# Rows of the moving operands 272 elements apart instead of 256, and the on-chip layout moved to make room

## The chip, the cores and the metric

The kernel runs on one core of one Trainium2 chip. Its time is the device time of one launch in microseconds (us). The kernel before takes 2373.92 us, the median of three runs (2372.8 to 2373.94).

## The reference, cut to what matters

Two transformer-like blocks in float32 on a sequence of 256 tokens with a model width of 2048. What costs time is a row of large products; everything between them is element-wise work on arrays of 256 columns.

```python
# first block, d = 2048, 256 tokens, 256 context tokens
mod = silu(c) @ w_mod                      # 2048 -> 6*2048 (and the same for c_ctx)
hx, hc = modulate(rms_norm(x), ...), modulate(rms_norm(ctx), ...)
q, zf, zb, v = split((hx | hc) @ w_in[:, :4096])      # "rec": both sequences
s_f, s_b = gated scan over the context                # states per head
g, sb, sc, sh, ga, gb = split(hx @ w_in[:, 4096:])    # "mix" and "merge"
y_a, y_b = scan output * silu(g), sb * short_conv(sc * sh)
merged = sigmoid(ga) * (y_a @ w_pa) + sigmoid(gb) * (y_b @ w_pb)   # "merge"
x = x + g1 * (merged @ w_o)                           # "out"
a, b = split(modulate(rms_norm(x)) @ w_up)            # "up", 2048 -> 2*5632
x = x + g2 * ((silu(dwconv3x3(a)) * b) @ w_down)      # "down", 5632 -> 2048
x = rms_norm(x)
# second block: 16 learned tokens put ahead, so 272 tokens
proj = rms_norm(h) @ w_in_2                           # "attn", 2048 -> 8*1024
mixed = [stick_breaking(q, k, v), diff_attention(q, k, v)] * silu(gates)
return h + mixed @ w_out_2                            # "proj"
```

## The kernel before, in words

Activations lie transposed: features on the 128 partitions, tokens along the row. A product of 128 output features is one pass over all blocks k of 128 input features (16 of them; 11 in a product of "down"), and its output is one [128, 256] tile in one of four PSUM banks (ACC).

To reach float32 accuracy, both operands are split into a high part (rounded by the float32r type) and a low part. SyncE loads the weights of a product (1 MB) into RAW, ScalarE copies RAW to HI (L455), VectorE writes LO = RAW - HI (L1135), each in two halves. For every k, `prod` (L744 and following; all its matmuls are recorded at L759) then issues three matmuls into the same bank: HI by the high part of the input, HI by the low part, LO by the high part. Each matmul record has its own weight load of 128 columns (PEld, also L759). The HI and LO tiles hold [2 slots, 16 blocks, 128], so one block of weights is 512 bytes further than the last.

The inputs of products ("moving" operands) are these tiles, with the high and the low part in different slots of the same tile:

- HX [128, 4, 16, 256]: hx and hc, high and low. "rec" reads both sequences at once, as two blocks of 256 columns (512 columns per matmul) for three products per head, and hx alone for the fourth; "mix", "merge" (two of three products) and "up" read hx.
- YAB [128, 4, 8, 256]: y_a and y_b, for the third product of "merge". MRG [128, 2, 16, 256] for "out". SH and SL [128, 44, 256] for "down". MIX [128, 2, 16, 256] for "proj".
- U2 [128, 2, 16, 272]: the input of "attn". Its rows are already 272 elements long. Four of the eight products of a head (p = 0, 3, 6, 7) read columns 16 to 272 of a row, the other four (1, 2, 4, 5) all 272.

The stages follow one another in the order of the list PHASES, as hardware loops: mod1 (vector by matrix, weights streamed), rec (8 heads of 4 products), mix (8 heads of 4), merge (16 columns of 3), out (16 products), up (88), down (64 products of 11 blocks), attn (8 heads of 8), proj (16). In rec, merge and out VectorE also does one unit each of `mod_unit` (L1145): a [128, 2048] multiply and sum straight from RAW.

A product waits for a free bank, for its LO halves and in some stages for its inputs. SyncE loads a weight unit as soon as the LO two units ahead of it has read the buffer. Every on-chip tile has a fixed address: `at(name, kb, shape)` gives it the offset base + kb * 1024 bytes, with base = 16512; so tiles of different stages lie over each other, and the order of the stages and semaphores keep them apart. The first 16 KB below are the scratch in which descriptors of DMAs that GpSimd issues are built. GpSimd issues six DMAs in all: 1 MB to the tensor park in HBM early on and back into CROWB ahead of merge, 2 MB of X1 to park after out, 2 MB back into XF and the 16 learned tokens when up has ended, and constants ahead of attn.

Of the kernel before, what the change touches and what calls it, by code (L numbers as in the profile page):

```python
# [8 lines left out]
F32R = mybir.dt.float32r  # L9
# [5 lines left out]
P = 128  # L15
# [107 lines left out]
def build(nc, xct, metat, crow, vec, con1, con2, wts, wdown, park, outt):  # L123
    ctx = ExitStack()
    with ctx:
        base = 16512

# [10 lines left out]

        HX = at("hx", 64, [P, 4, KD, T], F32R)
        YAB = at("yab", 96, [P, 4, HEADS, T], F32R)  # L140
        XC = at("xc", 128, [P, 2, KD, T])
        SQ1 = at("sq1", 160, [P, 2, 4, 2, T])
        SS1 = at("ss1", 194, [P, 2, T])
        RAWX = at("rawx", 48, [P, 2, 16, P])
        CS32 = at("cs32", 182, [P, KD, 32])
        ROW = at("row", 168, [P, 2, 4 * P])
        RS1 = at("rs1", 176, [P, 2, T])
        N1 = at("n1", 178, [P, 2, 2, T])
        FG = at("fg", 144, [P, 2, HEADS, T])
        VT = at("vt", 160, [P, 2, HEADS * P])  # L150
        ST = at("st", 168, [P, 2, HEADS, P])
        QF = at("qf", 176, [P, HEADS, T])
        MRG = at("mrg", 144, [P, 2, KD, T], F32R)
        X1 = at("x1", 128, [P, KD, T])
        SH = at("sh", 96, [P, FF, T], F32R)
        SL = at("sl", 140, [P, FF, T], F32R)
        XF = at("xf", 64, [P, KD, T])
        U2 = at("u2", 96, [P, 2, KD, TA], F32R)
        MIX = at("mix", 130, [P, 2, 2 * HEADS, T], F32R)
        CON2 = at("con2", 162, [P, NC2])  # L160

        CON1 = at("con1", 184 + 13.5, [P, NC1])
        cbase = 184 + 13.5 + NC1 / 256
        VEC = at("vec", cbase, [P, NVEC])
# [7 lines left out]

        SG = at("sg", 128, [P, 2, 2, T])
        FC = at("fc", 132, [P, 2, T])
        EXC = at("exc", 136, [P, 2, T])
        KDT = at("kdt", 138, [P, 4, P])
        VS = at("vs", 140, [P, 2, T])
        VCT = at("vct", 142, [P, 2, P])
        SGQ = at("sgq", 143, [P, T])
        ONE = at("one", 184, [P, T])  # L180

        CROW = at("crow_all", 185, [P, D])
        CROWB = at("crow_b", 176, [P, D])
        CGATE = at("cgate", 160, [P, D])

        AR = at("ar", 128, [P, 4, T])
        TT0 = at("tt0", 132, [P, 3, T])
        QK = at("qk", 135, [P, 4, T])
        QLA = at("qla", 139, [P, 2, 2, T])
        KS = at("ks", 143, [P, T])  # L190
        TT1 = at("tt1", 184, [P, 3, P])
        QLB = at("qlb", 185.5, [P, 1, 2, T])
        ON = at("on", 187.5, [P, 2, P])
        YT = at("yt", 188.5, [P, T])
        SC = at("sc", 189.5, [P, 2, T])
        QS = at("qs", 191.5, [P, 2, T])

        GS = at("gs", 193.5, [P, T])
        SGG = at("sgg", 194.5, [P, T])
        UP = at("up", 195.5, [P, T + 8])  # L200
        SCB = at("scb", cbase + 4.625, [P, T])

        GA = at("ga", 184, [P, T])
        GB = at("gb", 185, [P, T])
        M1 = at("m1", 186, [P, T])
        M2 = at("m2", 187, [P, T])

        SQ2 = at("sq2", 190, [P, 2, T])
        ZERO = at("zero", 196.25, [P, T])
        RS2 = at("rs2", 187, [P, T])  # L210
        N2 = at("n2", 188, [P, 8, T])

        AT = at("at", 184, [P, 6, GRID + 2])
        CV = at("cv", 185.75, [P, T])
        CV2 = at("cv2", 186.75, [P, T])
        S1 = at("s1", 187.75, [P, T])

        SQ3 = at("sq3", 192, [P, 2, 2, T])
        RSF = at("rsf", 190, [P, T])

# [3 lines left out]
        SQMS = at("sqms", 83, [P, NMETA])  # L224
        RTOK = at("rtok", 184, [P, TA])
        SGB = at("sgb", 185.25, [P, T])
        SGD = at("sgd", 186.25, [P, T])
        a0 = 80
# [10 lines left out]
        GDF = at("gdf", a0 + 14.5625, [P, T])  # L239
        b0 = 162 + NC2 / 256  # L240
        SS = at("ss", b0, [P, 2, P + NMETA + TA])
# [513 lines left out]
        def _(pe):  # L755
# [50 lines left out]
            pe.wait_ge(c_silu, 1)  # L806
            xch, xcl = (lambda k: HX[:, 0:3:2, k, :]), (lambda k: HX[:, 1:4:2, k, :])

# [30 lines left out]
            def rec_head(i, peeled):  # L839
# [5 lines left out]
                def turns():  # L845
# [9 lines left out]
                    for s in range(2):  # L855
# [3 lines left out]

                prod("rec", i, 6, lambda k: HX[:, 0, k, :], lambda k: HX[:, 1, k, :], lambda k: ACC[:, 3, 0:T],  # L860
                     between=turns)
# [60 lines left out]
            def mix_head(i, peeled):  # L922

                xh, xl = (lambda k: HX[:, 0, k, :]), (lambda k: HX[:, 1, k, :])

                prod("mix", i, 0, xh, xl, lambda k: ACC[:, 0, 0:T], between=None if peeled else lambda: mix_level(i - 1, 7))
                if not peeled:
                    mix_outputs(i - 1)
                mix_same(i)
                mix_level(i, 0)  # L930
                prod("mix", i, 1, xh, xl, lambda k: ACC[:, 1, 0:T], between=lambda: mix_level(i, 1))
                if not peeled:
                    mix_turn(i - 1)
# [9 lines left out]
            def merge_columns(i, peeled=False):  # L943

                xh, xl = (lambda k: HX[:, 0, k, :]), (lambda k: HX[:, 1, k, :])
                for jj in range(4):
# [7 lines left out]
                    if first:  # L954
                        mix_turn(HEADS - 1, True)
                        pe.wait_ge(yb_ready, 1 + HEADS)

                    prod("merge", i, p + 2, lambda k: YAB[:, 2 - 2 * (k // 8), k % 8, :], lambda k: YAB[:, 3 - 2 * (k // 8), k % 8, :],
                         lambda k: ACC[:, (b + 2) % 4, (1 - k // 8) * T:(2 - k // 8) * T], lambda k: (k % 8 == 0, k % 8 == 7),
# [8 lines left out]
            with pe.Fori(0, ITERS["out"]) as i:  # L968
# [5 lines left out]
                for jj in range(4):  # L974
                    prod("out", i, 2 * jj, lambda k: MRG[:, 0, k, :], lambda k: MRG[:, 1, k, :], lambda k: ACC[:, jj, 0:T],
                         between=lambda: squares(jj - 1), inputs=mrg_ready if jj == 0 else None, each=4)
# [3 lines left out]
            with pe.Fori(0, ITERS["up"]) as i:  # L980
                for p in range(4):
                    prod("up", i, p, lambda k: HX[:, 0, k, :], lambda k: HX[:, 1, k, :], lambda k: ACC[:, p, 0:T],
                         inputs=hx2_ready if p == 0 else None)
# [4 lines left out]
            with pe.Fori(0, ITERS["down"]) as i:  # L988
# [9 lines left out]
                for jj in range(2):  # L998
                    for q in range(4):
                        p = 4 * jj + q  # L1000
                        u = prod_index("down", i, p)
                        if jj == 0:
                            pe.wait_ge(s_hidden, 1 + DT * (q + 1))
                        prod("down", i, p, lambda k: SH[:, DT * q + k, :], lambda k: SL[:, DT * q + k, :],
                             lambda k: ACC[:, jj, 0:T], lambda k: (q == 0 and k == 0, q == 3 and k == DT - 1),
# [106 lines left out]
            with pe.Fori(0, ITERS["proj"]) as i:  # L1112
                for p in range(4):
                    prod("proj", i, p, lambda k: MIX[:, 0, k, :], lambda k: MIX[:, 1, k, :], lambda k: ACC[:, p, 0:T],
                         inputs=mix_ready, needs=head_order if p == 0 else {KD: 0})
# [3 lines left out]
        def _(dve):  # L1119
# [73 lines left out]
            def inputs(j):  # L1193

                dve.wait_ge(h1_aff, j + 1)
                hh, hl = HX[:, 0:3:2, j, :], HX[:, 1:4:2, j, :]
                link(V.tensor_copy(hh, N1[:, j % 2]))
# [102 lines left out]
            def mix_ya(i):  # L1300

                x = lambda d: YAB[:, d, bass.ds(i, 1), :].rearrange("p a t -> p (a t)")
                dve.wait_ge(on_tr, i + 1)
# [22 lines left out]
            def mix_head(i, peeled):  # L1326
# [26 lines left out]

                x = lambda d: YAB[:, d, bass.ds(i, 1), :].rearrange("p a t -> p (a t)")
                qf = QF[:, bass.ds(i, 1), :].rearrange("p a t -> p (a t)")
# [56 lines left out]
            def merge_columns(i, peeled=False):  # L1412

                for jj in range(4):
# [21 lines left out]
                    dve.wait_ge(bank_free, prod_index("merge", i, p + 2) + 1)  # L1436
                    o = lambda s: MRG[:, s, bass.ds(j, 1), :].rearrange("p a t -> p (a t)")
                    link(V.tensor_copy(o(0), M1[:]))
# [25 lines left out]
            for g in range(5):  # L1464
# [3 lines left out]
                if g > 0:  # L1468
                    n = N2[:, 4 * ((g - 1) % 2):4 * ((g - 1) % 2) + 4, :]
                    dve.wait_ge(h2_aff, g)  # L1470
                    split_small(HX[:, 0, 4 * g - 4:4 * g, :], HX[:, 1, 4 * g - 4:4 * g, :], n).then_inc(hx2_ready, 1)
                    dve.wait_ge(hx2_ready, g)
# [4 lines left out]
            with dve.Fori(0, ITERS["up"]) as i:  # L1477
                ch.enter(i, CHAIN["v_up"])
                for jj in range(2):
# [28 lines left out]
                    dve.wait_ge(bank_free, prod_index("up", i, 2 * jj + 1) + 1)  # L1508
                    o = lambda t: t[:, bass.ds(j, 1), :].rearrange("p a t -> p (a t)")
                    split_small(o(SH), o(SL), CV2[:]).then_inc(s_hidden, 1)  # L1510
# [82 lines left out]
            def attn_head(i, peeled):  # L1593
# [6 lines left out]
                def mixed(g):  # L1600
                    o = lambda s: MIX[:, s, bass.ds(2 * i + 1 - g, 1), :].rearrange("p a t -> p (a t)")
                    split_small(o(0), o(1), MT[:]).then_inc(mix_ready, 1)
# [222 lines left out]
```

## Time and profile before

| what | value |
|---|---|
| median of 3 runs | 2373.92 us |
| the profiled execution's own time | 2372.26 us |
| its span, first to last instruction | 2370.5 us |
| TensorE matmul busy | 2303.0 us, 97% of the span |
| VectorE, ScalarE busy | 1632.6 us (69%), 983.3 us (41%) |
| mean granted TensorE clock | 0.992 |
| DMA queues | 201 GB/s over the span |

A busy share is the share of the span in which at least one instruction of that engine was in work. Matmuls are pipelined: the duration of one (some 280 ns at 256 columns) is its time from start to modelled end, while the next one starts long before that. What a matmul costs in a stream is therefore the distance between two starts: divide a stretch by the number of matmuls in it.

Inside the span, rec runs in the window 137 to 421 us, mix in 455 to 655, merge in 672 to 945, out in 945 to 1044, up in 1062 to 1560, down in 1572 to 1834, attn in 1834 to 2275 and proj in 2275 to 2370; a window leaves the seams between stages out.

### The profile page before, as it was taken

How to read it: one execution, taken by the hardware profiler on the slowest of the kernel's cores; microseconds unless marked ns; L12 is line 12 of the kernel's file. 1: busy time of each engine (PE TensorE's matmuls, PEld its weight loads, DVE VectorE, ACT ScalarE, POOL GpSimd, SP SyncE). 2: the span in 40 equal slices, each digit the busy share in tenths (PEclk: the TensorE clock that was granted, in tenths of full speed). 3: DMA queues.
4: the chain of work that ended last, by engine and by line, in shares of the span. 5: the costliest groups of instructions: out<-in, count | busy, mean ns of one | idle time of the engine just before them, and what ended most of it. 6: DMA issues, size and time to landing. Idle time of an engine off the chain costs nothing.

```text
span 2370.5 us, 48809 instructions
## 1 busy us (share of the span) xinstructions
PE 2303.0 (97%) x18474; PEld 2221.4 (94%) x18474; DVE 1632.6 (69%) x2522; ACT 983.3 (41%) x1370; POOL 8.4 (0%) x18
## 2 busy tenths in 40 slices
PE   3899999999999999989999999999999999999999
PEld 2688888999999999989999999999999999999999
DVE  3465556999976666888888778864455766666764
ACT  4223222545533334344444444444344544444442
POOL 0000000000000000000000000000000000000000
PEclk8999999999999999999999999999999999999999
DMA  9965555433356667875444454455555444344443
GB/s 398 399 231 212 204 220 191 182 128 138 134 217 240 243 239 289 330 281 189 177 177 185 187 182 189 178 184 182 171 170 191 164 157 162 144 157 155 146 175 127
DMA packets 69511, 475.62 MB, mean 201 GB/s; under 512 B 7728, under 2 KB 9776, under 8 KB 18384
## 3 DMA queue, kind: packets, MB, share of 16 engines
q1 hardware_dynamic: 68688, 467.59, 52.6%
q0 software_dynamic: 768, 7.26, 0.8%
q8 instruction: 39, 0.64, 0.1%
q14 instruction: 16, 0.13, 0.0%
HBM read 469.58 MB, written 5.24 MB: 200 GB/s over the span
## 4 chain that ended last, share of the span: by engine, by line
PE 84%; DVE 8%; DMA 4%; issue 2%; ACT 1%; DVEq 1%; SPq 0%; ACTq 0%
PE acc L759 80%; PE aux L759 4%; DMA raw<-wts 4%; DVE lo L1135 3%; DVE ar L1352 2%; DVE qla L1345 1%; DVE sc L1324 1%; DVE tt L1350 1%; DVE qlb L1345 0%; PE aux L1030 0%; DVE yab L1151 0%; ACT hi L455 0%; DVE yab L1152 0%; DVE hx L1152 0%; ACT n L630 0%
## 5 line engine op out<-in xcount | busy, mean ns | idle before, releaser
L759 PE MATMUL acc<-hx,hi 128*128 128x256 f32 (+1 forms) x5888 | 1174.2, 299 | 11.5 <-DVE hx L1152 8.5
L759 PEld LDWEIGHTS acc<-hx,hi 128*128 128x128 f32 x5888 | 942.8, 192 | 45.8 <-issue 13.9
L1135 DVE TENSOR_TENSOR lo<-raw,hi 128x1024 fp32r<-128x1024 f32 (+1 forms) x716 | 811.1, 1167 | 218.7 <-ACT hi L455 214.4
L759 PE MATMUL acc<-hx,lo 128*128 128x256 f32 (+1 forms) x2944 | 875.1, 297 | 0.0
L455 ACT ACTIVATE hi<-raw 128x1024 fp32r<-128x1024 f32 (+1 forms) x716 | 694.6, 1010 | 330.0 <-PE acc L759 272.5
L759 PEld LDWEIGHTS acc<-hx,lo 128*128 128x128 f32 x2944 | 564.1, 192 | 15.6
L759 PE MATMUL acc<-u,hi 128*128 128x272 f32 (+1 forms) x2048 | 384.0, 288 | 0.0
L759 PEld LDWEIGHTS acc<-u,hi 128*128 128x128 f32 x2048 | 318.6, 188 | 4.5 <-issue 2.5
L759 PE MATMUL acc<-u,lo 128*128 128x256 f32 (+1 forms) x1024 | 291.6, 285 | 0.0
L759 PE MATMUL acc<-sh,hi 128*128 128x256 f32 x704 | 202.4, 288 | 0.4 <-DVE lo L1135 0.4
L759 PE MATMUL acc<-sh,lo 128*128 128x256 f32 x704 | 199.3, 283 | 0.0
L759 PE MATMUL acc<-sl,hi 128*128 128x256 f32 x704 | 199.2, 283 | 0.0
L759 PEld LDWEIGHTS acc<-u,lo 128*128 128x128 f32 x1024 | 193.0, 188 | 0.0
L759 PEld LDWEIGHTS acc<-sh,hi 128*128 128x128 f32 x704 | 135.1, 192 | 1.1 <-DVE lo L1135 0.6
L759 PEld LDWEIGHTS acc<-sl,hi 128*128 128x128 f32 x704 | 135.1, 192 | 0.4
L759 PEld LDWEIGHTS acc<-sh,lo 128*128 128x128 f32 x704 | 135.0, 192 | 0.0
L1501 DVE SCALAR_TENSOR_TENSOR cv<-at,vec,cv 128x256 f32<-128x256 f32 x308 | 129.1, 477 | 0.0
L759 PE MATMUL acc<-mrg,hi 128*128 128x256 f32 x512 | 95.7, 288 | 0.0
L759 PE MATMUL acc<-yab,hi 128*128 128x256 f32 x512 | 92.9, 283 | 0.0
L759 PE MATMUL acc<-mix,hi 128*128 128x256 f32 x512 | 92.3, 283 | 0.0
L759 PEld LDWEIGHTS acc<-mrg,hi 128*128 128x128 f32 x512 | 80.7, 191 | 0.9
L759 PEld LDWEIGHTS acc<-yab,hi 128*128 128x128 f32 x512 | 79.9, 192 | 0.2 <-issue 0.2
(286 smaller groups left out, 1979.1 us busy)
## 6 DMA issues: line engine op xcount, KB each, us to landing
raw<-wts SPq DMA_DIRECT2D x390, 1024.0 KB, 4.8
raw<-wdown SPq DMA_DIRECT2D x64, 704.0 KB, 4.1
xc<-xct SPq DMA_DIRECT2D x1, 4096.0 KB, 12.6
rawx<-wts SPq DMA_DIRECT2D x2, 1024.0 KB, 27.7
x<-xct SPq DMA_DIRECT2D x1, 2048.0 KB, 10.6
park<-x POOLq DMA_DIRECT2D x1, 2048.0 KB, 8.7
xf<-park POOLq DMA_DIRECT2D x1, 2048.0 KB, 10.6
outt<-outs SPq DMA_DIRECT2D x16, 128.0 KB, 3.9
```

The source lines that it names most:

```text
L455: A.activation(HI[:, slot, a:b, :], RAW[:, p % 4, a:b, :], ACT.Copy).then_inc(hi_half, 1)
L759: return pe.matmul(*a, **k)
L1135: V.tensor_tensor(LO[:, slot, a:b, :], RAW[:, p % 4, a:b, :], HI[:, slot, a:b, :].bitcast(F32), ALU.subtract).then_inc(lo_half, 1)
L1324: V.copy_predicated(SC4[:, 0:4:3, :], m, AUX[:, bank, 0:T].rearrange("p (t n) -> p t n", t=2)).then_inc(tile_read, 1)
L1345: V.tensor_tensor(q, ar, qk, ALU.mult).then_inc(ql_ready, 1)
L1350: mark(V.tensor_tensor(bass.AP(after[:].tensor, 0, [[3 * (P, T)[l % 2], P], [1, 3 * blocks // 2]]), even, odd, ALU.mult))
L1352: mark(V.tensor_tensor(ar, ar, tt, ALU.mult))
L1501: mark(V.scalar_tensor_tensor(acc4[n % 2], a, w, acc4[n % 2], ALU.mult, ALU.add))
```

## The change

All moving operands get rows of TW = 272 elements, of which only the first 256 are written and read. HX and YAB, MRG, MIX, SH and SL grow by a sixteenth each. "up" reads its input through a new name, HXU, of two slots over the same place as HX. To make the room, the scratch for DMAs of GpSimd is set to 8192 bytes (by default the base of 16512 left 16384), the base of all tiles goes 8192 bytes down, and most tiles after YAB get kb values 8 higher, so that their absolute addresses stay; X1, MRG, SL, AT, CV, CV2, S1 and ZERO go elsewhere. The loops, the order of instructions, the semaphores and the number and shape of all operations are the same.

```diff
+TW = T + NMETA
-        base = 16512
+        base = 8320
-        HX = at("hx", 64, [P, 4, KD, T], F32R)
-        YAB = at("yab", 96, [P, 4, HEADS, T], F32R)
-        XC = at("xc", 128, [P, 2, KD, T])
+        HX = at("hx", 64, [P, 4, KD, TW], F32R)
+        YAB = at("yab", 98, [P, 4, HEADS, TW], F32R)
+        XC = at("xc", 136, [P, 2, KD, T])
...
-        MRG = at("mrg", 144, [P, 2, KD, T], F32R)
-        X1 = at("x1", 128, [P, KD, T])
-        SH = at("sh", 96, [P, FF, T], F32R)
-        SL = at("sl", 140, [P, FF, T], F32R)
+        MRG = at("mrg", 150, [P, 2, KD, TW], F32R)
+        X1 = at("x1", 134, [P, KD, T])
+        HXU = at("hxu", 64, [P, 2, KD, TW], F32R)
+        SH = at("sh", 98, [P, FF, TW], F32R)
+        SL = at("sl", 144.75, [P, FF, TW], F32R)
         XF = at("xf", 64, [P, KD, T])
         U2 = at("u2", 96, [P, 2, KD, TA], F32R)
-        MIX = at("mix", 130, [P, 2, 2 * HEADS, T], F32R)
+        MIX = at("mix", 130, [P, 2, 2 * HEADS, TW], F32R)
...
-        ZERO = at("zero", 196.25, [P, T])
+        ZERO = at("zero", cbase + 4.625, [P, T])
-        AT = at("at", 184, [P, 6, GRID + 2])
+        AT = at("at", 200, [P, 6, GRID + 2])
...
-            xch, xcl = (lambda k: HX[:, 0:3:2, k, :]), (lambda k: HX[:, 1:4:2, k, :])
+            xch, xcl = (lambda k: HX[:, 0:3:2, k, 0:T]), (lambda k: HX[:, 1:4:2, k, 0:T])
...
-                    prod("up", i, p, lambda k: HX[:, 0, k, :], lambda k: HX[:, 1, k, :], lambda k: ACC[:, p, 0:T],
+                    prod("up", i, p, lambda k: HXU[:, 0, k, 0:T], lambda k: HXU[:, 1, k, 0:T], lambda k: ACC[:, p, 0:T],
...
-                    split_small(HX[:, 0, 4 * g - 4:4 * g, :], HX[:, 1, 4 * g - 4:4 * g, :], n).then_inc(hx2_ready, 1)
+                    split_small(HXU[:, 0, 4 * g - 4:4 * g, 0:T], HXU[:, 1, 4 * g - 4:4 * g, 0:T], n).then_inc(hx2_ready, 1)
...
-    nc = bacc.Bacc("TRN2", target_bir_lowering=False, num_devices=1)
+    nc = bacc.Bacc("TRN2", target_bir_lowering=False, num_devices=1, dynamic_dma_scratch_size=8192)
```

All other reads and writes of these tiles change in the same way, from `:` to `0:T`.

## Rows read from the trace of the kernel before

**Rows 1.** The page: busy time by engine; the chain that ended last, by engine.

```profile
PE 2303.0 (97%) x18474; PEld 2221.4 (94%) x18474; DVE 1632.6 (69%) x2522; ACT 983.3 (41%) x1370; POOL 8.4 (0%) x18
...
PE 84%; DVE 8%; DMA 4%; issue 2%; ACT 1%; DVEq 1%; SPq 0%; ACTq 0%
```

**Rows 2.** Windows: us, busy of PE, PEld, DVE, ACT, POOL, PEclk, DMA share, GB/s.

```profile
137.00:421.00 284.00, 284.00 (x1481) 244.40 (x1480) 168.33 (x215) 73.80 (x94) 0.00 (x0) 1.00 0.56 212
...
455.00:655.00 200.00, 193.82 (x1607) 190.38 (x1606) 189.91 (x340) 102.87 (x170) 3.16 (x6) 1.00 0.37 137
...
672.00:945.00 273.00, 272.71 (x2271) 272.32 (x2271) 176.33 (x208) 109.01 (x136) 0.00 (x0) 1.00 0.66 250
945.00:1044.00 99.00, 99.00 (x803) 98.11 (x802) 81.19 (x84) 37.17 (x47) 0.00 (x0) 1.00 0.89 334
...
1062.00:1560.00 498.00, 498.00 (x4151) 497.87 (x4150) 397.37 (x692) 221.43 (x305) 0.00 (x0) 1.00 0.48 180
...
1572.00:1834.00 262.00, 262.00 (x2135) 260.27 (x2134) 130.69 (x166) 109.62 (x155) 0.33 (x1) 1.00 0.53 182
1834.00:2275.00 441.00, 439.67 (x3465) 426.42 (x3463) 306.10 (x516) 207.06 (x302) 0.21 (x1) 1.00 0.41 155
```

**Rows 3.** The chain in order of time: start us, us, what (rec, merge, up, down, proj).

```profile
141.75 35.56 PE acc L759 x168
...
738.28 210.22 PE acc L759 x1752
...
1061.66 497.25 PE acc L759 x4140
...
1573.16 15.83 PE acc L759 x132
...
2275.54 92.36 PE acc L759 x768
```

**Rows 4.** Timeline of PE in "up": start us, us, instruction; twelve blocks k lie between.

```profile
1099.74 0.40 PE L759 MATMUL acc<-hx,hi 128*128 128x256 f32 x2
...
1104.06 0.40 PE L759 MATMUL acc<-hx,hi 128*128 128x256 f32 x2
```

**Rows 5.** Timeline of PE in "attn", seventh product (p = 6), blocks k = 9 to 15.

```profile
1933.70 0.40 PE L759 MATMUL acc<-u,hi 128*128 128x256 f32 x2
...
1934.06 0.40 PE L759 MATMUL acc<-u,hi 128*128 128x256 f32 x2
...
1934.41 0.40 PE L759 MATMUL acc<-u,hi 128*128 128x256 f32 x2
...
1934.77 0.40 PE L759 MATMUL acc<-u,hi 128*128 128x256 f32 x2
...
1935.83 0.40 PE L759 MATMUL acc<-u,hi 128*128 128x256 f32 x2
```

**Rows 6.** The same, first blocks of the product after a stop (p = 7).

```profile
1939.49 0.28 PE L759 MATMUL acc<-u,lo 128*128 128x256 f32 x1
...
1940.88 0.28 PE L759 MATMUL acc<-u,lo 128*128 128x256 f32 x1
```

**Rows 7.** The same, a product of 272 columns from column 0 (p = 2).

```profile
1957.79 0.41 PE L759 MATMUL acc<-u,hi 128*128 128x272 f32 x2
...
1958.92 0.42 PE L759 MATMUL acc<-u,hi 128*128 128x272 f32 x2
...
1959.31 0.41 PE L759 MATMUL acc<-u,hi 128*128 128x272 f32 x2
...
1963.46 0.42 PE L759 MATMUL acc<-u,hi 128*128 128x272 f32 x2
```

**Rows 8.** DVE between out and up, by shape: busy us, mean ns.

```profile
L1151 DVE CAST hx<-n 128x1024 fp32r<-128x1024 f32 x4 | 2.8, 690 | 1.4 <-ACT n L630 1.4
```

**Rows 9.** DMA issues of GpSimd: KB, us to landing; who DVE's L1557 waited for.

```profile
xf<-park POOLq DMA_DIRECT2D x1, 2048.0 KB, 10.6
...
DVE xf L1557 <- PE acc L759: 25.8, 15, 2.6
```

More of the change, by code:

```diff
@@ L137, in build @@
         LO = at("lo", 48, [P, 2, 16, P], F32R)
-        HX = at("hx", 64, [P, 4, KD, T], F32R)
-        YAB = at("yab", 96, [P, 4, HEADS, T], F32R)
-        XC = at("xc", 128, [P, 2, KD, T])
-        SQ1 = at("sq1", 160, [P, 2, 4, 2, T])
-        SS1 = at("ss1", 194, [P, 2, T])
-        RAWX = at("rawx", 48, [P, 2, 16, P])
[L145 to L152, printed above, removed]
-        MRG = at("mrg", 144, [P, 2, KD, T], F32R)
-        X1 = at("x1", 128, [P, KD, T])
-        SH = at("sh", 96, [P, FF, T], F32R)
-        SL = at("sl", 140, [P, FF, T], F32R)
+        HX = at("hx", 64, [P, 4, KD, TW], F32R)
+        YAB = at("yab", 98, [P, 4, HEADS, TW], F32R)
+        XC = at("xc", 136, [P, 2, KD, T])
+        SQ1 = at("sq1", 168, [P, 2, 4, 2, T])
+        SS1 = at("ss1", 202, [P, 2, T])
+        RAWX = at("rawx", 48, [P, 2, 16, P])
+        CS32 = at("cs32", 190, [P, KD, 32])
+        ROW = at("row", 176, [P, 2, 4 * P])
+        RS1 = at("rs1", 184, [P, 2, T])
+        N1 = at("n1", 186, [P, 2, 2, T])
+        FG = at("fg", 152, [P, 2, HEADS, T])
+        VT = at("vt", 168, [P, 2, HEADS * P])
+        ST = at("st", 176, [P, 2, HEADS, P])
+        QF = at("qf", 184, [P, HEADS, T])
+        MRG = at("mrg", 150, [P, 2, KD, TW], F32R)
[3 more added lines that the diff above has]
+        SL = at("sl", 144.75, [P, FF, TW], F32R)
         XF = at("xf", 64, [P, KD, T])
         U2 = at("u2", 96, [P, 2, KD, TA], F32R)
-        MIX = at("mix", 130, [P, 2, 2 * HEADS, T], F32R)
-        CON2 = at("con2", 162, [P, NC2])
-        CON1 = at("con1", 184 + 13.5, [P, NC1])
-        cbase = 184 + 13.5 + NC1 / 256
+        MIX = at("mix", 130, [P, 2, 2 * HEADS, TW], F32R)
+        CON2 = at("con2", 170, [P, NC2])
+        CON1 = at("con1", 192 + 13.5, [P, NC1])
+        cbase = 192 + 13.5 + NC1 / 256
         VEC = at("vec", cbase, [P, NVEC])
@@ L171, in build @@
         SMALL = at("small", cbase + 4.5, [P, 32])
[L173 to L200, printed above, removed]
@@ L201, in build @@
-        SCB = at("scb", cbase + 4.625, [P, T])
[L203 to L208, printed above, removed]
-        ZERO = at("zero", 196.25, [P, T])
-        RS2 = at("rs2", 187, [P, T])
-        N2 = at("n2", 188, [P, 8, T])
-        AT = at("at", 184, [P, 6, GRID + 2])
-        CV = at("cv", 185.75, [P, T])
-        CV2 = at("cv2", 186.75, [P, T])
-        S1 = at("s1", 187.75, [P, T])
@@ L218, in build @@
-        SQ3 = at("sq3", 192, [P, 2, 2, T])
-        RSF = at("rsf", 190, [P, T])
+        SG = at("sg", 136, [P, 2, 2, T])
+        FC = at("fc", 140, [P, 2, T])
+        EXC = at("exc", 144, [P, 2, T])
+        KDT = at("kdt", 146, [P, 4, P])
+        VS = at("vs", 148, [P, 2, T])
+        VCT = at("vct", 150, [P, 2, P])
+        SGQ = at("sgq", 151, [P, T])
+        ONE = at("one", 192, [P, T])
+        CROW = at("crow_all", 193, [P, D])
+        CROWB = at("crow_b", 184, [P, D])
+        CGATE = at("cgate", 168, [P, D])
@@ new lines, in build @@
+        AR = at("ar", 136, [P, 4, T])
+        TT0 = at("tt0", 140, [P, 3, T])
+        QK = at("qk", 143, [P, 4, T])
+        QLA = at("qla", 147, [P, 2, 2, T])
+        KS = at("ks", 151, [P, T])
+        TT1 = at("tt1", 192, [P, 3, P])
+        QLB = at("qlb", 193.5, [P, 1, 2, T])
+        ON = at("on", 195.5, [P, 2, P])
+        YT = at("yt", 196.5, [P, T])
+        SC = at("sc", 197.5, [P, 2, T])
+        QS = at("qs", 199.5, [P, 2, T])
+        GS = at("gs", 201.5, [P, T])
+        SGG = at("sgg", 202.5, [P, T])
@@ new lines, in build @@
+        UP = at("up", 203.5, [P, T + 8])
+        SCB = at("scb", cbase + 4.625, [P, T])
+        GA = at("ga", 192, [P, T])
+        GB = at("gb", 193, [P, T])
+        M1 = at("m1", 194, [P, T])
+        M2 = at("m2", 195, [P, T])
+        SQ2 = at("sq2", 198, [P, 2, T])
+        ZERO = at("zero", cbase + 4.625, [P, T])
+        RS2 = at("rs2", 195, [P, T])
+        N2 = at("n2", 196, [P, 8, T])
+        AT = at("at", 200, [P, 6, GRID + 2])
+        CV = at("cv", 201.75, [P, T])
+        CV2 = at("cv2", 202.75, [P, T])
@@ L221, in build @@
+        S1 = at("s1", 203.75, [P, T])
+        SQ3 = at("sq3", 200, [P, 2, 2, T])
+        RSF = at("rsf", 198, [P, T])
         METT = at("mett", 80, [P, KD, NMETA])
@@ L224, in build @@
         SQMS = at("sqms", 83, [P, NMETA])
-        RTOK = at("rtok", 184, [P, TA])
-        SGB = at("sgb", 185.25, [P, T])
-        SGD = at("sgd", 186.25, [P, T])
+        RTOK = at("rtok", 192, [P, TA])
+        SGB = at("sgb", 193.25, [P, T])
+        SGD = at("sgd", 194.25, [P, T])
         a0 = 80
@@ L239, in build @@
         GDF = at("gdf", a0 + 14.5625, [P, T])
-        b0 = 162 + NC2 / 256
+        b0 = 170 + NC2 / 256
         SS = at("ss", b0, [P, 2, P + NMETA + TA])
@@ L858, in turns @@
                     ins.then_inc(v_tr, 1)
-                prod("rec", i, 6, lambda k: HX[:, 0, k, :], lambda k: HX[:, 1, k, :], lambda k: ACC[:, 3, 0:T],
+                prod("rec", i, 6, lambda k: HX[:, 0, k, 0:T], lambda k: HX[:, 1, k, 0:T], lambda k: ACC[:, 3, 0:T],
                      between=turns)
@@ L922, in mix_head @@
             def mix_head(i, peeled):
-                xh, xl = (lambda k: HX[:, 0, k, :]), (lambda k: HX[:, 1, k, :])
+                xh, xl = (lambda k: HX[:, 0, k, 0:T]), (lambda k: HX[:, 1, k, 0:T])
                 prod("mix", i, 0, xh, xl, lambda k: ACC[:, 0, 0:T], between=None if peeled else lambda: mix_level(i - 1, 7))
@@ L943, in merge_columns @@
             def merge_columns(i, peeled=False):
-                xh, xl = (lambda k: HX[:, 0, k, :]), (lambda k: HX[:, 1, k, :])
+                xh, xl = (lambda k: HX[:, 0, k, 0:T]), (lambda k: HX[:, 1, k, 0:T])
                 for jj in range(4):
@@ L956, in merge_columns @@
                         pe.wait_ge(yb_ready, 1 + HEADS)
-                    prod("merge", i, p + 2, lambda k: YAB[:, 2 - 2 * (k // 8), k % 8, :], lambda k: YAB[:, 3 - 2 * (k // 8), k % 8, :],
+                    prod("merge", i, p + 2, lambda k: YAB[:, 2 - 2 * (k // 8), k % 8, 0:T], lambda k: YAB[:, 3 - 2 * (k // 8), k % 8, 0:T],
                          lambda k: ACC[:, (b + 2) % 4, (1 - k // 8) * T:(2 - k // 8) * T], lambda k: (k % 8 == 0, k % 8 == 7),
@@ L974, in _ @@
                 for jj in range(4):
-                    prod("out", i, 2 * jj, lambda k: MRG[:, 0, k, :], lambda k: MRG[:, 1, k, :], lambda k: ACC[:, jj, 0:T],
+                    prod("out", i, 2 * jj, lambda k: MRG[:, 0, k, 0:T], lambda k: MRG[:, 1, k, 0:T], lambda k: ACC[:, jj, 0:T],
                          between=lambda: squares(jj - 1), inputs=mrg_ready if jj == 0 else None, each=4)
@@ L1003, in _ @@
                             pe.wait_ge(s_hidden, 1 + DT * (q + 1))
-                        prod("down", i, p, lambda k: SH[:, DT * q + k, :], lambda k: SL[:, DT * q + k, :],
+                        prod("down", i, p, lambda k: SH[:, DT * q + k, 0:T], lambda k: SL[:, DT * q + k, 0:T],
                              lambda k: ACC[:, jj, 0:T], lambda k: (q == 0 and k == 0, q == 3 and k == DT - 1),
@@ L1113, in _ @@
                 for p in range(4):
-                    prod("proj", i, p, lambda k: MIX[:, 0, k, :], lambda k: MIX[:, 1, k, :], lambda k: ACC[:, p, 0:T],
+                    prod("proj", i, p, lambda k: MIX[:, 0, k, 0:T], lambda k: MIX[:, 1, k, 0:T], lambda k: ACC[:, p, 0:T],
                          inputs=mix_ready, needs=head_order if p == 0 else {KD: 0})
@@ L1195, in inputs @@
                 dve.wait_ge(h1_aff, j + 1)
-                hh, hl = HX[:, 0:3:2, j, :], HX[:, 1:4:2, j, :]
+                hh, hl = HX[:, 0:3:2, j, 0:T], HX[:, 1:4:2, j, 0:T]
                 link(V.tensor_copy(hh, N1[:, j % 2]))
@@ L1300, in mix_ya @@
             def mix_ya(i):
-                x = lambda d: YAB[:, d, bass.ds(i, 1), :].rearrange("p a t -> p (a t)")
+                x = lambda d: YAB[:, d, bass.ds(i, 1), 0:T].rearrange("p a t -> p (a t)")
                 dve.wait_ge(on_tr, i + 1)
@@ L1352, in level @@
                     mark(V.tensor_tensor(ar, ar, tt, ALU.mult))
-                x = lambda d: YAB[:, d, bass.ds(i, 1), :].rearrange("p a t -> p (a t)")
+                x = lambda d: YAB[:, d, bass.ds(i, 1), 0:T].rearrange("p a t -> p (a t)")
                 qf = QF[:, bass.ds(i, 1), :].rearrange("p a t -> p (a t)")
@@ L1436, in merge_columns @@
                     dve.wait_ge(bank_free, prod_index("merge", i, p + 2) + 1)
-                    o = lambda s: MRG[:, s, bass.ds(j, 1), :].rearrange("p a t -> p (a t)")
+                    o = lambda s: MRG[:, s, bass.ds(j, 1), 0:T].rearrange("p a t -> p (a t)")
                     link(V.tensor_copy(o(0), M1[:]))
@@ L1508, in _ @@
                     dve.wait_ge(bank_free, prod_index("up", i, 2 * jj + 1) + 1)
-                    o = lambda t: t[:, bass.ds(j, 1), :].rearrange("p a t -> p (a t)")
+                    o = lambda t: t[:, bass.ds(j, 1), 0:T].rearrange("p a t -> p (a t)")
                     split_small(o(SH), o(SL), CV2[:]).then_inc(s_hidden, 1)
@@ L1600, in mixed @@
                 def mixed(g):
-                    o = lambda s: MIX[:, s, bass.ds(2 * i + 1 - g, 1), :].rearrange("p a t -> p (a t)")
+                    o = lambda s: MIX[:, s, bass.ds(2 * i + 1 - g, 1), 0:T].rearrange("p a t -> p (a t)")
                     split_small(o(0), o(1), MT[:]).then_inc(mix_ready, 1)
```

## The prediction

> **What bounds the kernel now.** I read the page first: TensorE is busy in 97% of the span, and 84% of the chain that ended last is its work [rows 1]. The windows by stage then say where that is a limit and where it is only company [rows 2]. In rec, merge, out, up, down and attn TensorE is busy in nearly all of the stretch while VectorE is busy in half to just over four fifths of it (in up 397 of 498 us, in out 81 of 99). In mix TensorE is busy 193.8 of 200 us, but VectorE is busy 189.9 of the same 200, in 340 short instructions that depend on one another: I read it as VectorE setting the pace there. DMA is far from full but for out, with 334 GB/s in a share of 0.89.
>
> So the figure that matters is the distance between the starts of two matmuls in a stream. The chain gives it: 210.22 us for 1752 matmuls in merge, 120.0 ns; 497.25 for 4140 in up, 120.1; 15.83 for 132 in down, 119.9; 92.36 for 768 in proj, 120.3 with its last drain [rows 3]. In "up" twelve blocks of three take 4.32 us, 120.0 ns each [rows 4]. Four stages with quite different work on the other engines and different DMA traffic have one and the same figure, so neither those engines nor the DMAs set it. What a column costs comes from rec: 168 matmuls in 35.56 us, of which 144 have 512 columns and 24 have 256; 35.56 less 24 x 0.120 is 32.68, over 144 is 226.9 ns [rows 3]. So 256 columns more cost 106.9 ns, 0.418 ns each, one column per cycle of the 2.4 GHz level (granted clock 1.00 in these windows [rows 2]). A matmul of 256 columns at 120.0 ns thus carries 13.0 ns that are not columns. The change can only touch these.
>
> **The change, part by part.**
>
> *The pitch.* The kernel before has the case already: U2 has rows of 272 elements, everything else rows of 256. In attn, matmuls of 256 columns from U2, well inside a product, take 2.13 us for 18, 118.3 ns [rows 5]. They are the same instructions as in up: three per block, same weights tiles, same banks, same clock. The steps between blocks show more: 0.36, 0.35, 0.36 us, where up has 0.36 on the mean of twelve [rows 4, 5]. At 256 elements (1024 bytes) each row starts at the same place modulo any smaller power of two, as the weights do, which lie 512 bytes apart; at 272 (1088 bytes) each row starts 64 bytes further against the weights. I take the 13.0 ns to be in part a clash between the stream of the input and the load of the next weights that depends on their relative place, and the 1.7 ns to be what walking through four places (64 bytes x 4 = 256) gains on standing at the worst or near it.
>
> The new reads start at column 0, those of U2 at column 16, that is 64 bytes on: one step of the walk. Over four blocks they visit the same places. The distance from high to low slot, 16 x 1088 bytes in HX, is a multiple of 256 as in U2; for SH to SL it is 46.75 KB, also one; 8192 bytes off all bases changes nothing in this count. So I put the rate of rows 5 on all changed tiles.
>
> Other rows bound it. After a stop, the first blocks from U2 run at 1.39 us for 12, 115.8 ns [rows 6]: gain 4.2. Products of 272 columns from column 0 take 5.67 us for 45, 126.0 ns [rows 7]; less 16 columns at 0.418 that is 119.3: gain 0.7. The latter starts at column 0 as the new reads do but is longer, the former reading is of the right length; I take 1.7 because length decides when the next load falls into the stream, and the start is only a shift of the walk. The inner ends are 0.7 and 4.2.
>
> *How many matmuls.* From the loops: rec 8 x 48 = 384 of 256 columns and 8 x 144 = 1152 of 512; merge 16 x 3 x 48 = 2304; out 768; up 88 x 48 = 4224; down 64 x 33 = 2112; proj 768. That is 10,560 of 256 columns. Mix has 1536 more, which I count at nothing: VectorE's chain covers them, and a quicker product there only makes TensorE wait longer [rows 2]. For the 512-column ones no row has the new pitch; the load is hidden behind the same one matmul, so I give them the same 1.7 (ends: 0 and 4.2, since twice the columns may halve or double what clashes). Attn keeps its tile, its reads and, modulo 256, its address: nothing.
>
> Sum: 10,560 x 1.7 = 18.0 us, by stage: up 7.2, merge 3.9, down 3.6, out 1.3, proj 1.3, rec 0.7. And 1152 x 1.7 = 2.0. Together 20.0 us.
>
> A sentence of the Trainium skill speaks against this. Its page "SBUF — State Buffer", section "Who interferes with whom", gives TensorE two independent read ports, one for the moving operand and one for weight loads, and says that TensorE never waits on anyone. By it the pitch could not matter, and the time would stay. The trace doesn't sit well with that: 120.0 against 118.3 ns for the same instruction with only the tile's pitch and start different [rows 4, 5].
>
> *What is late next.* At 118.3 ns a pair of products of up takes 11.36 us instead of 11.52. VectorE is busy 397 of 498 us there, 9.2 us per pair; it keeps 2 us of slack. Out loads 2 MB per column: 334 GB/s become 339. Nothing else comes near.
>
> *VectorE and ScalarE.* Writes to the tiles by single rows keep their shape. Between out and up four copies of 1024 elements go into HX as four rows now with holes; they take 690 ns each [rows 8]. If holes cost them a faster mode they would take up to twice that, 4 x 0.7 = 2.8 us on the path, since TensorE waits there; copies into two separate blocks exist elsewhere, so I take 0, ends 0 and 2.8.
>
> *The halved scratch.* Only six DMAs of GpSimd use it. The one with least room is xf from park: 10.6 us to landing [rows 9], issued at the end of up, needed after the first four products of down, about 4 x 4 = 16 us later; in the trace VectorE waits there for TensorE and not for the DMA [rows 9]. Should the smaller ring force the DMA into two turns, 21 us instead of 10.6 would make it late by 5 us, once. I take 0, ends 0 and 5.
>
> Total: 2372.26 - 20.0 = 2352.3 for an execution like the profiled one (span 2370.5 and 1.8 around it). The median lies 1.66 higher, so 2354.0.
>
> **The rivals.**
>
> (a) *The weaker reading of the pitch*: 0.7 ns a matmul, as rows 7 give it. 11,712 x 0.7 = 8.2 us: 2365.7. For it: these rows start at column 0. Against: rows 5 are the same shape as the new ones.
>
> (b) *No change*: the 1.7 ns belong to something else in attn, say stops of the queue that let weight loads run ahead. For it: after a stop the rate is better [rows 6], and attn has many stops. Against: rows 5 lie nine blocks and more after the last stop, and down, where each column of products has a stop in it, is back at 119.9 within a product [rows 3]. Time 2373.9.
>
> (c) *Slower*: the walk through the places isn't an average that wins but has a bad step, and the new tiles sit in it more than U2 does. In rows 7 the step from 1958.92 to 1959.31 is 130 ns a matmul, 123.3 after taking off 16 columns: 3.3 ns over the standing 120. If the changed tiles had that step throughout, 11,712 x 3.3 = 39 us: 2413; it decides from a mean above 120.0 on. For it: one step in four is that long. Against: four steps together are still under 120 in both shapes of attn, and the new tiles walk the same four.
>
> (d) *More*: streams from column 0 keep the rate of rows 6 all the way: 11,712 x 4.2 = 49 us, 2325. Nothing but the first blocks after a stop shows it.
>
> **How the numbers follow.** Forecast (gain 1.2 to 2.6 ns, 2343 to 2360) 0.60; (a) 0.14; (d) or a part of it 0.09; (b) 0.10; (c) or a ring or copy that costs more than the pitch gives 0.07. A measurement of this kernel tells a change from none at about 0.2%, 4.7 us; so faster has 0.60 + 0.14 + 0.09 = 0.83, same 0.10, slower 0.07. The range leaves out (b) and (c) at 0.17 and the far part of (d): 2335 to 2369.
>
> **What would show it.** Right: the chain's stretches in up, merge, down and proj come to 118 to 118.5 ns a matmul, with steps between blocks that alternate; attn's stretches stay as they are; mix keeps its length, with a little more waiting of TensorE; copies at L1151 stay at 690 ns; L1557 still waits for TensorE. Wrong: up at 120.0 (then pitch isn't the cause), or up quicker and attn slower (then it is the base), or mix shorter too (then VectorE wasn't its limit).

## The result, and the profile after

The changed kernel takes 2360.11 us (median of 5, 2359.81 to 2360.93) against 2373.47 for the kernel before (2372.59 to 2373.94): a ratio of 0.9946 with a 95% interval of 0.9932 to 0.9959, 13.4 us less. The forecast was 2354.0, 20 us less, with 2335 to 2369 as its range. The direction was right and the gain is two thirds of what was forecast. The time alone lies between the forecast and rival (a), 2365.7; the rates per matmul below tell the two apart.

The chain of waits of the changed kernel, in order of time (start us, us, what), answers to [rows 3]. A line of it is called a piece below: a stretch of TensorE's work with no wait in it that the profile shows.

```profile
142.01 36.18 PE acc L761 x168
...
742.02 207.32 PE acc L761 x1752
...
1061.57 490.37 PE acc L761 x4140
...
1566.07 15.62 PE acc L761 x132
...
2265.20 91.09 PE acc L761 x768
```

Divide again: merge 118.3 ns a matmul (120.0 before), up 118.4 (120.1), down 118.3 (119.9), proj 118.6 (120.3). But rec, whose pieces of 168 hold 144 matmuls of 512 columns, went the other way: 36.18 us instead of 35.56. Less 24 of 118.3 ns, the 512-column ones take 231.5 ns; before it was 226.9.

The start times of the same pieces tell how the difference to before builds up: +0.3 us at the first of rec, +3.7 at the long one of merge, -0.1 at that of up, -7.1 at the first of down, -10.3 at proj, and -11.6 at the end of the span (2358.9 against 2370.5). The medians lie 13.4 apart; these two traces hold 11.6 of it. The seven pieces of 168 in rec lose 7 x 0.62 = 4.3 us, mix is as long as it was, and the start of merge gives 0.9 back by the second of these marks; the rest of merge and out give 3.8, up 7.0, down and attn 3.3, proj 1.3. Attn itself stays as it was: 436.8 us from its first piece to the start of proj's in both kernels.

The timeline of TensorE in up, blocks twelve apart and two between (start us, us, instruction), answers to [rows 4]. Three matmuls make a block; the steps now alternate as those of U2 did in [rows 5], and twelve of them take 4.26 us, 118.3 ns each:

```profile
1099.85 0.40 PE L761 MATMUL acc<-hxu,hi 128*128 128x256 f32 x2
...
1100.20 0.40 PE L761 MATMUL acc<-hxu,hi 128*128 128x256 f32 x2
...
1100.56 0.40 PE L761 MATMUL acc<-hxu,hi 128*128 128x256 f32 x2
...
1104.11 0.40 PE L761 MATMUL acc<-hxu,hi 128*128 128x256 f32 x2
```

The groups by shape between out and up, then VectorE's waits and GpSimd's DMAs, answer to [rows 8, 9]. The copies keep their 690 ns, the waits at the place where xf is needed still name TensorE, and the DMA takes 10.9 us:

```profile
L1153 DVE CAST hxu<-n 128x1024 fp32r<-128x1024 f32 x4 | 2.8, 690 | 1.4 <-ACT n L632 1.4
```

```profile
DVE xf L1559 <- PE acc L761: 24.7, 15, 2.5
```

```profile
xf<-park POOLq DMA_DIRECT2D x1, 2048.0 KB, 10.9
```

### The profile page after: what moved, and what is told of

Its sections match the earlier page's. It is cut to its first block, busy times and chain, and to the rows that moved or that the text cites. A ratio compares the mean times of both kernels' runs of the same rounds, so it can differ in the third digit from the quotient of the medians.

```text
span 2358.9 us, 48809 instructions
## 1 busy us (share of the span) xinstructions
PE 2291.3 (97%) x18474; PEld 2203.9 (93%) x18474; DVE 1633.4 (69%) x2522; ACT 984.5 (42%) x1370; POOL 8.4 (0%) x18
## 4 chain that ended last, share of the span: by engine, by line
PE 84%; DVE 9%; DMA 4%; issue 2%; ACT 1%; DVEq 1%; SPq 0%; ACTq 0%
PE acc L761 79%; PE aux L761 4%; DMA raw<-wts 4%; DVE lo L1137 3%; DVE ar L1354 2%; DVE qla L1347 1%; DVE sc L1326 1%; DVE tt L1352 1%; DVE qlb L1347 0%; PE aux L1032 0%; ACT hi L457 0%; DVE yab L1153 0%; DVE yab L1154 0%; DVE hxu L1154 0%; ACT n L632 0%
## 5 line engine op out<-in xcount | busy, mean ns | idle before, releaser
L761 PE MATMUL acc<-hx,hi 128*128 128x256 f32 (+1 forms) x3072 | 663.4, 312 | 2.8 <-DVE lo L1137 2.3
L761 PEld LDWEIGHTS acc<-hx,hi 128*128 128x128 f32 x3072 | 497.7, 189 | 39.7 <-issue 5.3
L761 PE MATMUL acc<-hxu,hi 128*128 128x256 f32 x2816 | 502.0, 281 | 8.4 <-DVE hxu L1154 8.2
L761 PE MATMUL acc<-hx,lo 128*128 128x256 f32 (+1 forms) x1536 | 476.2, 310 | 0.0
L761 PEld LDWEIGHTS acc<-hxu,hi 128*128 128x128 f32 x2816 | 433.5, 189 | 9.5 <-issue 8.2
L761 PE MATMUL acc<-hxu,lo 128*128 128x256 f32 x1408 | 396.8, 282 | 0.0
L761 PEld LDWEIGHTS acc<-hx,lo 128*128 128x128 f32 x1536 | 291.0, 189 | 16.6
L761 PEld LDWEIGHTS acc<-hxu,lo 128*128 128x128 f32 x1408 | 267.4, 190 | 0.0
## 6 DMA issues: line engine op xcount, KB each, us to landing
x<-xct SPq DMA_DIRECT2D x1, 2048.0 KB, 10.3
xf<-park POOLq DMA_DIRECT2D x1, 2048.0 KB, 10.9
```

The lines of the kernel that those rows point to most:

```text
L761: return pe.matmul(*a, **k)
```

## The experiments

The question was what of the pitch matters: that rows walk, or where they stand against the weights. Below, the "place" of a tile is the distance in bytes of its row starts from the row starts of HI and LO, modulo 256. Rows 256 elements apart all have one place; rows of 272 walk over 0, 64, 128 and 192. Experiments 1 to 6, 8 to 10 and 12 were run once each, so what they say is read from the lengths of their pieces, and not from a few us of the total.

**1. Base alone.** `base = 8320` and the halved scratch, all rows still 256 elements.

> The kernel before with the halved scratch and all tiles 8192 bytes lower, rows still 256 elements. Theory A (the pitch alone moved the time): 256-column matmuls stand at 120.0 ns in up, 512-column ones at 226.9 in rec, time within 0.1% of before, 2373 us. Theory B (the base or the smaller scratch does part of it): rec gets longer by up to 5 us or up gets quicker already here.

Measured 2373.7 us, with 2373.28 for the kernel before beside it; up 497.25 us for 4140 matmuls as before. Theory B falls: base and scratch change nothing that can be seen.

**2 and 3. A constant shift.** As 1, with rows of 256 elements, and every tile but the four of the weights 64 or 128 bytes on. (The edit for 64 bytes; base and scratch as in 1 are left out.)

```diff
-            return nc.alloc_sbuf_tensor_at(name, shape, dt, offset=base + int(kb * 1024))
+            return nc.alloc_sbuf_tensor_at(name, shape, dt, offset=base + int(kb * 1024) + (0 if name in ("raw", "hi", "lo", "rawx") else 64))
```

> As e1, and every tile but RAW, HI, LO and RAWX lies 64 bytes further, so that every moving row of 256 elements starts 64 bytes (modulo 256) from where the weights' rows start. Theory A1 (the relative place of stream and weight load sets the cost): all 256-column matmuls of hx, sh, sl, mrg, yab and mix leave 120.0 ns together and stand at one new figure between 113 and 122; at 118.3 the time is about 2354, and the 512-column ones move as well. Theory C (walking from row to row matters, a constant shift doesn't): 120.0 and 226.9 as before, 2373 us.

> As e2 with 128 bytes. Theory A1: another constant figure than at 0 and at 64 bytes; the mean over the four places 0, 64, 128 and 192 should lie near the 118.3 of the walk, so with 120.0 at 0 at least one of 64 and 128 is under 118.3. Theory C: 120.0 and 2373 us.

Measured 2351.31 and 2368.01 us against 2373.28. Without any change of pitch, 64 bytes give 22 us, more than the change itself. Theory C (only walking matters) falls. The first piece of rec and the long one of up, at 64 bytes:

```profile
141.62 35.69 PE acc L759 x168
...
181.91 35.80 PE acc L759 x168
...
1056.24 488.08 PE acc L759 x4140
```

and at 128 bytes:

```profile
144.85 36.30 PE acc L759 x168
...
1066.41 491.75 PE acc L759 x4140
```

Up stands at 117.9 and 118.8 ns. Rec is longer at both.

**4. The weights moved along.** As 2, with RAW, HI, LO and RAWX 64 bytes on too.

> As e2, but RAW, HI, LO and RAWX are moved by the same 64 bytes, so that nothing changes in relation. Theory A1 (relative place): 120.0 and 226.9 again, 2373 us. Theory D (the absolute place of the stream matters, not that of the weights): the same figures as in e2.

Measured 2372.57 us; all is as before:

```profile
142.02 35.56 PE acc L759 x168
...
1061.94 497.25 PE acc L759 x4140
```

So it is not the address of the moving rows but their distance from the weight tiles. Theory D falls. With experiment 2 this is the central pair of this case. It doesn't tell yet which of the shifted tiles counts, since those of the other engines moved too; experiments 7 and 10 do, below.

**5, 6, 8 and 9. More places.** The same edit with 192, 32, 224 and 160 bytes.

> The kernel before (rows of 256 elements) with the halved scratch, all tiles but RAW, HI, LO and RAWX 192 bytes further. Constant places 0, 64 and 128 gave 120.0, 117.7 and about 118.7 ns for a matmul of 256 columns. Theory A1 (a walk costs the mean of its four places, 118.3): 192 bytes must give 4 x 118.3 - 120.0 - 117.7 - 118.7 = 116.8 ns, time 2373 - 10560 x 3.2 = about 2340, unless the 512-column ones get worse. Rival A2 (the order of the places in a walk has a cost of its own, so that no mean holds): another figure, 118 to 120.

> As e5 with 32 bytes. Theory A3 (only the place in units of 64 bytes counts): 120.0 as at 0, or 117.7 as at 64. Theory A4 (a finer pattern): a figure of its own between or beside them. No forecast of the sign beyond that; 2351 to 2374.

> As the 192-byte run, with 224 bytes. Constant places gave in up 120.0 (0), 116.7 (32), 117.8 (64), 118.7 (128) and 113.3 ns (192), in rec 226.9, 233.3, 229.2, 232.4 and 233.3. If the cost follows the place smoothly, 224 lies between 113.3 and 120.0 in up and the time between 2327 and 2374; if it is a pattern with jumps, anything, 113.3 or 120.0 among it.

> As above with 160 bytes, between 128 (118.7) and 192 (113.3). Smooth: about 116 ns in up, 2345 us. In jumps: 113.3 or over 118.

Measured 2326.71, 2345.98, 2362.76 and 2368.73 us (2373.24 and 2372.24 for before beside them). The chain at 192 bytes (rec, merge, up, two products' stretches of down, proj):

```profile
182.63 36.34 PE acc L759 x168
...
740.51 206.35 PE acc L759 x1752
...
1057.31 469.76 PE acc L759 x4140
...
1540.90 15.55 PE acc L759 x132
...
1557.32 14.98 PE acc L759 x132
...
2235.09 87.27 PE acc L759 x768
```

and the piece of up at 32, 224 and 160 bytes:

```profile
1058.00 483.50 PE acc L759 x4140
```

```profile
1064.02 490.37 PE acc L759 x4140
```

```profile
1068.34 491.75 PE acc L759 x4140
```

| place, bytes | 0 | 32 | 64 | 128 | 160 | 192 | 224 | walk (the change) |
|---|---|---|---|---|---|---|---|---|
| up, ns a matmul (piece / 4140) | 120.1 | 116.8 | 117.9 | 118.8 | 118.8 | 113.5 | 118.4 | 118.4 |
| rec, us per 168 | 35.56 | 36.40 | 35.69 to 35.80 | 36.30 | 36.58 | 36.34 to 36.44 | 36.44 | 36.18 |
| total, us | 2373.7 | 2346.0 | 2351.3 | 2368.0 | 2368.7 | 2326.7 | 2362.8 | 2360.1 |

Place 0, where the kernel before stood, is the worst in up for 256 columns and the best of all for 512. Places 32 bytes apart differ, so theory A3 falls. The relation is not smooth: 160 costs what 128 does, and nothing between 128 and 192. The expectation that a walk costs the mean of its four places failed as well (117.6 from 120.1, 117.9, 118.8 and 113.5; it costs 118.4).

The table's row for up is one stage in one execution per place, and a place does not fix the rate by itself. At 160 bytes other stages of the same execution ran at other rates: merge at 120.0 ns, as at place 0, proj at 117.6, and the pieces of down in turn at 117.3, 120.0 and twice 118.6:

```profile
746.63 210.24 PE acc L759 x1752
...
1574.26 15.49 PE acc L759 x132
...
1590.61 15.84 PE acc L759 x132
...
2274.02 90.32 PE acc L759 x768
```

It is not the clock: rec, merge, up, down and proj have a granted clock of 1.00 in every trace. The other places but 0 and 224 show it too. At 64 bytes the 24 matmuls of 256 columns that end a piece of rec come at 113.3 ns in one head and at 117.9 in the next, which is the difference between its 35.69 and 35.80 us (below: the first of them and the instruction behind the last, in the two heads). At 128 the first piece of down took 15.84 us and the others 15.66; at 32 proj took 118.0 ns where up took 116.8.

```profile
174.43 0.39 PE L759 MATMUL acc<-hx,hi 128*128 128x256 f32 x2
...
177.15 0.60 PE L851 MATMUL aux<-con,exc 128*128 128x128 f32 x4
...
214.72 0.40 PE L759 MATMUL acc<-hx,hi 128*128 128x256 f32 x2
...
217.55 0.60 PE L851 MATMUL aux<-con,exc 128*128 128x128 f32 x4
```

At 192 bytes the modelled duration of a matmul is shorter as well. The groups by shape in up (1100 to 1500 us: busy us, mean ns), 192 bytes first, then the kernel before:

```profile
L759 PE MATMUL acc<-hx,hi 128*128 128x256 f32 x2354 | 400.2, 276 | 0.0
...
L759 PEld LDWEIGHTS acc<-hx,hi 128*128 128x128 f32 x2354 | 354.6, 188 | 0.0
```

```profile
L759 PE MATMUL acc<-hx,hi 128*128 128x256 f32 x2224 | 400.4, 283 | 0.0
...
L759 PEld LDWEIGHTS acc<-hx,hi 128*128 128x128 f32 x2223 | 346.8, 192 | 0.0
```

A matmul lasts 276 ns instead of 283, a weight load 188 instead of 192: about as much as the 6.7 ns between the two rates lies within the matmul's own duration, and at place 0 the load is longer too. A clash of the two would look like this, but the ends of matmuls are modelled, so these rows don't show it.

**7. HX alone back to 256 in the changed kernel.** Up reads through HXU, whose rows stay at 272.

```diff
-        HX = at("hx", 64, [P, 4, KD, TW], F32R)
+        HX = at("hx", 64, [P, 4, KD, T], F32R)
```

> The changed kernel with HX alone back at rows of 256 elements (place 0); all other tiles keep 272. If the 512-column matmuls of rec are what the change loses (231.7 against 226.9 ns by its trace), rec shortens by 4.9 us against the change, merge, whose products of hx stand at 120.0 again, gets longer by 1536 x 1.7 = 2.6, mix stays: 2357.8 against 2360.1 of the change. Rival (the loss in rec comes from the base or from the tiles moved with it): rec stays as long as in the change and the time is 2362 to 2363.

Measured 2358.84 us (2358.81 to 2359.43), ratio to before 0.9941 (0.9924 to 0.9958). Expected were 2357.8. Rec is back, and merge is 1.9 us longer, as its products of hx at the old rate should make it:

```profile
141.83 35.56 PE acc L761 x168
...
738.29 209.24 PE acc L761 x1752
...
1059.78 490.38 PE acc L761 x4140
```

From piece to piece of the two kernels, the long one of merge starts 3.7 us earlier than in the change and that of up 1.8 us earlier. The loss in rec comes from the reads of HX at the new pitch, nothing else that moved.

**10 and 11. Each tile at its better place.** Rows of 256 elements; HX at place 0 for rec, mix and merge, a name HXU of its own, 192 bytes further on, for up, and all other tiles but those of the weights at 192. (Base and scratch as in 1, and the reads and writes of up, which go to HXU, are left out.)

```diff
+            return nc.alloc_sbuf_tensor_at(name, shape, dt, offset=base + int(kb * 1024) + (0 if name in ("raw", "hi", "lo", "rawx", "hx") else 192))
...
+        HXU = at("hxu", 64, [P, 2, KD, T], F32R)
```

> HX at place 0 (rec, mix, and the products of hx in merge), its use in up and all other moving tiles at place 192, rows of 256 elements. If places act tile by tile: rec as before (512 columns at 226.9, 358 us in all against 363 at 192), merge's 1536 matmuls of hx at 120.0 again where 192 bytes had 116 on the mean (6 us more), up at 113.3, total within 2 us of the 2326.7 of the 192-byte run. Rival: the 113.3 ns of up hang on all tiles standing alike, then up falls back to 117 or more and the time is over 2340.

> The kernel of the tenth run again (HX at place 0, all other moving tiles at place 192, rows of 256), timed against the kernel before in five rounds. From its one time, 2322.93 against 2372.24: ratio 0.979, 2323 us. Its gain over the change (2360.1) should come from up (483 against 504 us), down, rec, merge, out and proj.

The tenth run gave 2322.93 us, 3.8 under the fifth, where at most 2 were expected: merge did not get longer (206.25 us for the piece, against 206.35), because its products of YAB ran at 113.6 ns here and nearly all at 117.8 in the fifth. Every tile but HX stands here as in the fifth run, and rec is back at 35.53 us; so the place of the tile that TensorE reads counts, not that of the other engines' tiles.

Timed in the eleventh: 2324.26 us (median of 6) against 2372.45, ratio 0.9811 with a 95% interval of 0.9788 to 0.9835. This version beats the kernel before by 48 us and, by the medians, the change by 36. But one of its six executions took 2342.73 us, where the others took 2322.7 to 2326.5. Up alone at 117.8 instead of 113.3 ns would give 4224 x 4.5 = 19 us more, an estimate that fits the 18; no trace of that execution was kept, so its cause is not shown. The gain of place 192 is thus not certain in every execution.

The chain in rec, merge, up and proj of an execution of 2323.2 us:

```profile
141.58 35.53 PE acc L760 x168
...
737.00 206.25 PE acc L760 x1752
...
1053.79 469.76 PE acc L760 x4140
...
2231.57 87.27 PE acc L760 x768
```

**12. Two rates at one place.** In down of the eleventh kernel the stretches between two sums of squares alternate, 15.55 and 14.98 us for the same 132 matmuls:

```profile
1569.63 15.55 PE acc L760 x132
...
1586.05 14.98 PE acc L760 x132
```

Its timeline shows where the rate changes, 113 ns before the two matmuls that are inserted for the squares, 118 behind (the four records of x4 are these two):

```profile
1535.33 0.28 PE L760 MATMUL acc<-sh,hi 128*128 128x256 f32 x1
...
1536.01 0.28 PE L760 MATMUL acc<-sh,hi 128*128 128x256 f32 x1
...
1536.36 1.02 PE L760 MATMUL aux<-sq,onesr 128*128 128x256 f32 x4
1537.03 0.47 PE L760 MATMUL acc<-sh,hi 128*128 128x256 f32 x1
1537.33 0.28 PE L760 MATMUL acc<-sl,hi 128*128 128x256 f32 x1
...
1537.57 0.28 PE L760 MATMUL acc<-sh,hi 128*128 128x256 f32 x1
...
1538.28 0.28 PE L760 MATMUL acc<-sh,hi 128*128 128x256 f32 x1
```

Two blocks ahead of it take 0.68 us, 113.3 ns a matmul; two behind it 0.71, 118.3 (117.8 over the whole piece). Experiment 12 takes the insertion out and keeps its waits; the last norm then lacks these sums, which come after down:

```diff
-                    for m in range(2):
-                        ins = mm(AUX[:, m, 0:T], ONESR[:], SQ3[:, n % 2, m, :], start=False, stop=False)
-                    ins.then_inc(ss3_mm, 1)
+                    pe.sem_inc(ss3_mm, 1)
```

> As the eleventh, but in down the two matmuls that sum squares (AUX, ONESR by SQ3) after the first half of the second and sixth product of an iteration are left out, their waits and semaphores kept; the second norm's sums are thus incomplete. In the tenth run the rate at place 192 in down was 113.3 ns up to that point, 117.6 behind it, and 113.3 again behind the next. Theory (the rate has two lasting states, and the insertion moves it from one to the other): down stands at 113.3 throughout, 16 insertions of some 0.19 us and half of 2112 x 4.2 ns less, so down 252 to 253 us against 259, total 2315 to 2317. Rival (the data or the k count sets the state): down keeps the alternation, and only some 3 us go, 2320.

Measured 2306.56 us. Down is one piece of 113.5 ns a matmul:

```profile
1535.75 235.43 PE acc L760 x2075
```

So the block count doesn't set the rate; the inserted matmuls move it from one lasting state to the other. Merge in the fifth run has the same: 113.3 ns ahead of a matmul inserted at 739.92 us, 117.8 from there to its end. The time fell by more than expected, since I had priced an insertion at 0.19 us: the timeline above has 0.67 us from the first inserted matmul to the next product's and 0.30 instead of 0.11 for that one, 0.86 in all. 16 x 0.86 is 13.8 us, and half of 2112 x 4.5 ns is 4.8; together 18.6. From the start of up to the start of attn's first piece the two traces differ by 18.2 us, the two times (2324.26 less 2306.56) by 17.7.

## Why the prediction was right, and where it was off

*The limit.* Right: TensorE's stream. In merge, out, up, down and proj each piece that got quicker per matmul carried its gain to the end.

*The price, 118.3 ns from U2.* Right to the tenth, 118.3 in merge, down and up's timeline, and not by luck: it was read from the same walk at the same shape. That the start column would only shift the walk held; rival (a) with its 119.3 and (b) with 120.0 did not come. By stage: up 7.0 (forecast 7.2), merge and out 4.7 (5.2), down 3.3 (3.6), proj 1.3 (1.3).

*Mix at nothing.* Right: between rec and merge nothing was gained though each product there got shorter. *Copies, ring, attn at nothing.* Right: 690 ns a copy, 10.9 us for the DMA against 10.6, attn's 436.8 us in both [rows 8, 9 and their answers]; experiment 1 shows it for the ring and the base.

*The 512-column matmuls.* This is the step that failed. I gave them the gain of the 256-column ones, 1.7 ns, with ends of 0 and 4.2, because "the load is hidden behind the same one matmul". They lost 4.6 ns each: 1152 x 6.3 is 7.3 us. The whole miss is 6.1 us by the medians (2354.0 and 2360.1) and 8.3 by the profiled executions (2352.3 and 2360.65), where the other stages together are 1.0 short of the forecast. No row had that shape at that pitch, and the ends should have reached below nothing: if a clash depends on the relative place, a shape for which the old place is good can lose by moving. The runs show just that: at each other place tried (experiments 2, 3, 5, 6, 8 and 9) rec is longer, and with HX alone back it is as before (7).

*The mechanism.* The relative place was right (experiments 2 and 4). "Walking over four places gains on standing at the worst" is half right: in up 0 is the worst for 256 columns, but the walk is no mean, and standing at 192 was better than walking by 5 ns. So the pitch of 272 was not needed for the gain. By the sentence of the Trainium skill ("SBUF — State Buffer", "Who interferes with whom") that TensorE's two read ports are independent and that it waits for nobody, the time would have stayed. The runs don't agree with that: moving one tile by 64 bytes against the other takes up from 120.1 to 117.9 ns for identical instructions. Whether it is at these ports that they meet no run shows.

*Left open.* That weight load and stream clash is argued from experiments 2 and 4 and the durations, not shown: HI and LO were always moved together with RAW, and the engines that write them were never taken out. Not tried either: whether the pattern repeats after 256 bytes, why one place has several lasting rates and which one a stage falls into, and what the remaining 6.4 ns over the columns are. With several rates at a place, a table with one value for each cannot rule out that another place would do as well as 192; at 64 bytes 113.3 ns were seen too. The places between those of the table were not run.

## What to carry to other kernels

When a stream of matmuls runs at one constant figure above its columns whatever the other engines do, shift the moving tiles against the weight tiles by some tens of bytes and measure each place; it costs no instruction, and here it was worth 1.9% by the median. Do it for every shape of matmul by itself, as the best place of one was the worst of another. Look at every stage, and at several executions, since one place gave more than one rate. And where a row of the trace has the new condition for one shape only, let the range for the other shapes reach to both sides.

## What the runs showed of the hardware that I had not expected

At a granted clock of 1.00, the same 256-column matmul with its own weight load comes every 113.3 to 120.0 ns, depending on the distance in bytes between its two operands' tiles and on what ran before; the 512-column one comes every 227 to 234 ns. At a distance of 192 bytes there are two lasting rates, 113.3 and 117.8 ns, and two small matmuls in between switch from one to the other; at 160 bytes there are at least three, 117.3, 118.6 and 120.0. An inserted pair of 256-column matmuls of plain float32 (the sums of squares) costs 0.86 us of TensorE's time, four times what 512 columns come to at 0.418 ns (0.21 us).
